# A transformer block with 32 experts: another row order of the down matrices, and the hidden units turned by eight 64x64 products

## What is computed

```python
hid = jax.nn.silu(t @ w_up1[e]) * (t @ w_up3[e])   # [rows, 512]
y = y + combine[:, e:e + 1] * (hid @ w_down[e])     # w_down[e] is [512, 1024]
```

## Time and profile before

| | us |
|---|---|
| median of 3 runs | 1080.02 (1079.77 to 1081.62) |
| profiled execution, its own time | 1080.52 |
| its span | 1078.4 |
| mean granted TensorE clock, share of full speed | 0.993 |
| TensorE matmul busy | 1026.4 (95%) |
| VectorE busy | 665.4 (62%) |
| packets of the SyncE queue, share of 16 DMA engines | 61.8% |

### The profile page before, as it was taken

The page is one execution under the profiler, slowest core; times in us unless marked ns, Lnnn a source line. Parts: engine busy times, 40 slices in busy tenths (PEclk is TensorE's granted clock), DMA queues, the critical chain, the costliest instruction groups (busy, mean ns, idle before and its releaser), DMA issues.

```text
span 1078.4 us, 18748 instructions
## 1 busy us (share of the span) xinstructions
PE 1026.4 (95%) x7675; PEld 590.0 (55%) x7675; DVE 665.4 (62%) x1132; ACT 326.0 (30%) x501; POOL 169.3 (16%) x220
## 2 busy tenths in 40 slices
PE   3899999999999999999999899999999999999995
PEld 1578577765556677777886344444434444444332
DVE  2478769355447543217627777777777777776666
ACT  3352462375553234336443110111111111101114
POOL 0100000233330101335700211111111000111003
PEclk9899999999999999999999999999999999999998
DMA  9666403203421004216327999999999999999994
GB/s 341 255 221 216 169 1 125 92 18 124 143 73 53 3 4 131 71 56 255 159 100 290 409 415 418 420 420 421 420 420 420 419 420 421 419 420 420 421 421 188
DMA packets 69717, 275.28 MB, mean 255 GB/s; under 512 B 9726, under 2 KB 19240, under 8 KB 45082
## 3 DMA queue, kind: packets, MB, share of 16 engines
q1 hardware_dynamic: 62976, 263.87, 61.8%
q10 hardware_dynamic: 2218, 6.52, 1.6%
q0 software_dynamic: 4464, 4.02, 1.1%
HBM read 282.42 MB, written 4.21 MB: 266 GB/s over the span
## 4 chain that ended last, share of the span: by engine, by line
PE 55%; SPq 14%; DVE 14%; DMA 8%; ACT 5%; issue 2%; POOL 1%; DVEq 0%; ACTq 0%
PE ps L2220 13%; SPq L479 9%; PE ps L2239 7%; PE ps L2204 4%; DMA ring<-in_w_in 3%; PE ps L1884 3%; SPq L483 3%; DMA arena<-in_w_up 3%; PE ps L1865 2%; PE ps L2198 2%; DMA arena<-in_w_mod 2%; PE ps L1873 2%; PE ps L1985 1%; PE ps L1866 1%; PE ps L1867 1%
## 5 line engine op out<-in xcount | busy, mean ns | idle before, releaser
L1550 DVE TENSOR_TENSOR arena<-arena,ps 128x1024 f32<-128x1024 f32 x124 | 145.3, 1212 | 38.6 <-PE ps L2204 38.6
L2220 PE MATMUL ps<-arena 128*64 128x512 f32 x672 | 152.6, 596 | 2.7 <-DMA arena<-in_w_up 2.4
L2220 PEld LDWEIGHTS ps<-arena 128*64 128x64 f32 x672 | 46.8, 137 | 95.1 <-issue 92.2
L1058 ACT ACTIVATE results<-ps,ST 64x512 fp32r<-64x512 f32 x64 | 43.7, 683 | 179.8 <-PE ps L2239 179.4
L2220 PE MATMUL ps<-ring,arena 128*64 128x512 f32 x352 | 79.8, 596 | 2.7 <-DVE arena L1508 1.4
L1051 ACT ACTIVATE arena<-ps 128x256 f32<-128x256 f32 x32 | 12.3, 384 | 218.9 <-PE ps L2220 218.9
L1726 PE MATMUL ps<-h_upper,w_upper 128*128 128x512 f32 (+1 forms) x184 | 73.9, 402 | 4.6 <-POOL h_lower_first L607 4.2
L2239 PE MATMUL ps<-arena 128*64 128x512 f32 x336 | 76.7, 598 | 0.0
L1560 DVE SCALAR_TENSOR_TENSOR results<-ps,ST,results 64x512 fp32r<-64x512 f32 x64 | 48.0, 750 | 44.7 <-ACT results L1058 44.2
L2204 PE MATMUL ps<-results,back 128*128 128x512 f32 x248 | 73.9, 419 | 0.0
L1728 PE MATMUL ps<-h_upper,w_lower 128*128 128x512 f32 (+1 forms) x184 | 72.4, 394 | 0.0
(11 more groups left out here) (426 smaller groups left out, 1868.1 us busy)
## 6 DMA issues: line engine op xcount, KB each, us to landing
arena<-in_w_up SPq DMA_DIRECT2D x84, 1024.0 KB, 24.7
ring<-in_w_up SPq DMA_DIRECT2D x44, 1024.0 KB, 24.1
ring<-in_w_down SPq DMA_DIRECT2D x11, 2048.0 KB, 25.5
arena<-in_w_down SPq DMA_DIRECT2D x11, 2048.0 KB, 26.6
arena<-in_w_down SPq DMA_DIRECT2D x20, 1024.0 KB, 24.4
ring<-in_w_mod SPq DMA_DIRECT2D x6, 2048.0 KB, 9.0
arena<-in_w_mod SPq DMA_DIRECT2D x6, 2048.0 KB, 9.8
ring<-in_w_in SPq DMA_DIRECT2D x6, 2048.0 KB, 8.2
```

Of the source, the lines that this page charges most:

```text
L1550: TT(two_banks(acc[:, t, :]), two_banks(acc[:, t, :]), ps[:, BACK_BANK[t]:BACK_BANK[t] + 2, :], ALU.add).then_inc(back_added, 1)
L2220: last = mm(ps[64 * hf:64 * hf + 64, UP_BANK, :].rearrange("p (m n) -> p m n", m=2), hgT[:, k, :], up_pair(u, k)[:, :, 256 * hf:256 * hf + ...
```

## The change

The down matrices are read as 4 rows per partition in one piece: partition p holds rows 4p to 4p+3. In sets 0 and 1 this is one DMA of 2 MB with 16 KB per partition in one piece. In set 2 it stays two DMAs of 1 MB, each with 8 KB per partition, now 16 KB apart in memory. The hidden units must then be turned so that partition p holds units 4p to 4p+3: for each residue j of the column modulo 4 and each half of the partitions (a = 0 and 64), one float32 product of the 64x64 block of `hid` with the 64x64 block of the identity on the diagonal. Eight such products take the place of the two transposes. Both products of a pair lie on the diagonal: rows a to a+63 of the array give PSUM partitions a to a+63. The wait for `hid_ready` is now taken by a raise of `register_pass`. `hidT` is read with k = 0 to 3 in order. The copy of it and all other instructions are as before. The new file is one line shorter above `expert_down`, so L2204 becomes L2203 and L2220 becomes L2219; the products that turn stand in L2228 and the down products in L2241.

```diff
-        dn = w_down.rearrange("o e (h p j) n -> p (o e) h (j n)", p=P, j=2)
+        dn = w_down.rearrange("o e (p j) n -> p (o e) (j n)", j=4)
...
             elif u < 2:
-                src = dn[:, bass.ds(e, 1), :, :].rearrange("p a k n -> p (a k) n")
-                dst = [ring[:, 2, :], S(6, 2)][u].rearrange("p (h n) -> p h n", h=2)
-                eng.dma_start(dst, src).then_inc(w_in_sem[u][m], 16)
+                src = dn[:, bass.ds(e, 1), :].rearrange("p a n -> p (a n)")
+                eng.dma_start([ring[:, 2, :], S(6, 2)][u], src).then_inc(w_in_sem[u][m], 16)
             else:
-                src = dn[:, bass.ds(e, 1), :, :].rearrange("p a k n -> p (a k) n")
                 for i in range(2):
-                    eng.dma_start(eset_down[u][i], src[:, i, :]).then_inc(w_in_sem[u][m], 16)
+                    src = dn[:, bass.ds(e, 1), 2 * D * i:2 * D * i + 2 * D].rearrange("p a n -> p (a n)")
+                    eng.dma_start(eset_down[u][i], src).then_inc(w_in_sem[u][m], 16)
...
             def expert_down(u, it, before):
                 pe.wait_ge(hid_ready, NSET * it + (u + 1))
-                for j in range(2):
-                    last = tr(ps[:, 1, P * j:P * j + P], hid.rearrange("p (n j) -> p j n", j=2)[:, j, :], ident)
+                pe.sem_inc(register_pass, 1)
+                for j in range(4):
+                    for a in (0, 64):
+                        last = mm(ps[a:a + 64, 1, 64 * j:64 * j + 64], hid.rearrange("p (n j) -> p j n", j=4)[a:a + 64, j, :],
+                                  ident[a:a + 64, a:a + 64], start=True, stop=True)
                 last.then_inc(ht_done, 1)
...
-                hv2 = hidT.rearrange("p (j h s) -> p j h s", j=2, h=2)
+                hv2 = hidT.rearrange("p (k s) -> p k s", k=4)
...
-                        last = mm(ps[64 * hf:64 * hf + 64, DOWN_BANK, :], hv2[:, k % 2, k // 2, :],
+                        last = mm(ps[64 * hf:64 * hf + 64, DOWN_BANK, :], hv2[:, k, :],
```

More of the change, by code:

```diff
@@ L543, in _ @@
             first = lambda i, m: esrc[i][:, bass.ds(2, 1), 2048 * m:2048 * m + 2048].rearrange("p a n -> p (a n)")
-            first_down = dn[:, bass.ds(2, 1), :, :].rearrange("p a k n -> p (a k) n")
+            first_down = dn[:, bass.ds(2, 1), :].rearrange("p a (k n) -> p (a k) n", k=2)
             sp.wait_ge(x1_ready, 2 * NT)
```

## The result

The changed kernel takes 1107.49 us (median of 4 runs, 1107.01 to 1110.64), the kernel before 1080.55 us beside it: a ratio of 1.0255, 95% interval 1.0233 to 1.0277. It is slower, as forecast, but by 26.9 us where 8.1 us were predicted, and outside the range. The profiled execution took 1110.64 us with a span of 1108.3 us, the mean clock was 0.987.

What follows compares the result with a forecast made beforehand. Loads and TensorE were both nearly full, the loads setting the end by 5.7 us. 31 units at 0.44 us plus 0.2 for unit 0, minus 5.7, gave +8.1 us: 1088.1 us median, range 1079.5 to 1093 us.

Steps and rivals of the forecast that it cites:

- The bounds: Whole expert stage: loads lose 1.2 us per unit against TensorE, run out of lead at 970 us, then cost 5.7 us.
- Part 1, the loads: Down loads of sets 0 and 1: 16 KB pieces save 0.1 us per load, 2 us less DMA time over 20 loads.
- The raise, +0.07 us: Before the turning: the raise takes over the wait for `hid`, 0.12 us to the weight load instead of 0.05.
- The turning, +0.37 us: From its first weight load to that of the next instruction: 0.60 us with eight products, against 0.23 before.
- the choice of L1985 over L1974: Pricing the turning by the mixer's diagonal pairs, 0.117 us per pair of products, not by four quarters at half of that.
- 7 x 0.058 us: Within the turning: seven steps between pairs of records, 0.41 us to the last pair.
- The last step: End of the turning: from the last pair to the next full-array weight load, 0.15 us, taken from L1962 after L1985.
- The copy of `hidT` hidden: After the turning: VectorE's copy ends at 811.11 us, ahead of the down products shifted to 811.71, so it adds nothing.
- The fourth: Rival on the turning: each product pays for its own weight load, 0.9 us per unit, 1102 us; chance 0.04.
- The third: Rival on the down loads: 16 KB pieces are slow, 20 loads cost 75 us, end near 1150 us; chance 0.05.
- The first: Rival on the turning: nearly free, 0.2 us per unit or less, loads set the end, 1078 to 1081 us; chance 0.12.
- The rule on drains: At the turning's end: changing tiling mode drains TensorE; without a drain 0.09 us less per unit, forecast 2.8 us lower.

Runs made afterwards that it cites:

- `columns_no_raise`: The changed kernel with eight products of 128 rows by 64 columns, still read with steps of 4, and no raise of `register_pass`: 1103.38 us, ratio 1.0199.

## Why the prediction was wrong

By its steps:

- **The bounds.** Right. Loads and TensorE were 5.7 us apart and TensorE had 0.18 us per unit to spare. The raise alone (0.06 us, no loss seen), the loads alone (1.6 us gained of at most 5.7) and the vanished waits after the change agree with it.
- **Part 1, the loads.** Right within the noise: 2 us of DMA time were estimated, the median fell by 1.6 us (0.3 to 2.6); with the turning they stay out of the sum.
- **The raise, +0.07 us.** Right: 0.12 us from the end of `hid` to the weight load, and 0.06 us per unit by itself.
- **The turning, +0.37 us.** This step failed. Its mechanism, the choice of L1985 over L1974 and the way of adding up were right for contiguous blocks: 0.64 us measured for 0.60. The term "7 x 0.058 us" was mis-sized, by a factor of two. In the changed kernel a pair of records takes 0.120 us, so 7 x 0.120 = 0.84 us, 0.43 more. L1985 stood for the new code because it has the pattern of array parts; that the new code reads its weights with steps of 4 elements was in the diff, and no row with such a step was looked for. The last step, from the last pair to the next full weight load, took 814.37 - 814.12 = 0.25 us instead of 0.15, another 0.1 us. Together 0.53 us more: 0.44 + 0.53 = 0.97 us per unit.
- **The copy of `hidT` hidden.** Right.
- **The sum.** 31 x 0.97 + 0.7 - 5.7 = +25.1 us in place of +8.1; unit 0 paid 0.7 us instead of 0.2. The remaining 1.8 us of the median are as much as unit 0's down products lost at a lower clock in the profile. The unprofiled runs have no records, so whether that is the same stays open.
- **Rivals.** The fourth named a turning of 0.9 us, 1102 us, at a chance of 0.04, and came nearest, but its reason was not the one: each product pays for its own weight load in contiguous blocks as well, and takes 0.058 us. The third fell: 16 KB pieces are not slow. The first fell too: even on four quarters and without steps the eight products take 0.42 us against 0.23, and a unit 0.25 us more.
- **The rule on drains.** The Trainium skill (TensorEngine Tiling (Array Packing), Key Properties) has the change of tiling mode drain TensorE. The step behind the last 64x64 record agrees with it: 0.15 us to the next full weight load without steps in the weights, 0.21 us with them, where records within the group follow every 0.06 and 0.12 us. The rule does not tell which forms pay. The eight 128x64 products of `columns_no_raise` pay the same 0.21 us at full height, while behind the four 128x64 transposes no extra step shows: the next weight load comes 0.11 us behind the last one. The step was in the sum at 0.15 us, so it is a small part of the miss.
- **Range and chances.** The dear end of the range (1093 us) was built from another 0.15 us per step between forms. No bound covered the one property in which the new operands differ from those of every row used. At twice L1985's pace that bound would have been 1101 us, and with the dear step on top 1105 us.

## What to carry to other kernels

When a row of another line prices a new instruction, compare the layout of its operands as well as its form: steps, not only rows, columns and array parts. It showed in products with 64 moving columns, and hardly in transposes with 128. If an order has to be changed with steps, the cheapest place here was a read of PSUM by ScalarE or VectorE (nothing), then a scattered write by VectorE (0.18 us for 256 columns), then the moving side of a large product (5%), then the weights of a small one (twice the time). And a saving on one of two nearly equal bounds is worth at most their distance, here 5.7 us of 1080.

## What the runs showed of the hardware

- A weight load of 64 float32 columns takes 134 ns contiguous, 135 ns with steps of 2 and 210 ns with steps of 4 elements; in 64x64 products, records on the same part of the array follow every 0.06 us (steps of 1 and 2) and every 0.12 us (steps of 4). In transposes with 128 moving columns (0.108 us each) the difference nearly vanishes. Steps of 3 and steps above 4 were not tried.
- Moving columns read in pairs, every other pair left out, made float32 products of 512 columns 5% longer.
- VectorE wrote 256 columns to places 64 elements apart, four by four, in 0.596 us instead of 0.42; reading PSUM with steps of 4 cost neither VectorE (0.420 us) nor ScalarE (0.383 us against 0.384) anything.
- Eight 64x64 products over four quarters take 0.42 us to the next full weight load, on the diagonal 0.64 us.
